# State-space scan: one direction's decay rows by broadcast transfers and a VectorE bound, the other's by TensorE products

## The reference

```
    acum = jnp.cumsum(loga.reshape(bsz, nc, CHUNK, ng, r), axis=2)
...
    alast = acum[:, :, -1]
    wgt = jnp.exp(alast[:, :, None] - acum)
...
        return (jnp.exp(al_c)[..., None, None] * s
                + jnp.einsum('bjgn,bjgr,bjgrp->bgrnp', bm_c, wgt_c, v_c))
...
    seg = jnp.exp(jnp.where(tril, acum[:, :, :, None] - acum[:, :, None], -jnp.inf))
    cb = jnp.einsum('bcign,bcjgn->bcijg', cm, bm)
    y_intra = jnp.einsum('bcijgr,bcjgrp->bcigrp', seg * cb[..., None], v)
    cdec = jnp.exp(acum)
...
        y = jnp.einsum('bign,bgrnp->bigrp', cm_c, s) * cd_c[..., None]
```

## Time and profile before

| | |
|---|---|
| median of 3 runs | 2175.74 us (2174.65 to 2176.6) |
| the profiled execution's own time | 2172.17 us |
| its span in the trace | 2170.4 us |
| PE busy | 1881.5 us (87%) |
| DVE busy | 805.8 us (37%) |
| ACT busy | 508.4 us (23%) |
| POOL busy | 333.5 us (15%) |

### The profile page before, as it was taken

The page is one execution under the profiler, slowest core; times in us unless marked ns, Lnnn a source line. Parts: engine busy times, 40 slices in busy tenths (PEclk is TensorE's granted clock), DMA queues, the critical chain, the costliest instruction groups (busy, mean ns, idle before and its releaser), DMA issues.

```text
span 2170.4 us, 32842 instructions
## 1 busy us (share of the span) xinstructions
PE 1881.5 (87%) x13986; PEld 1128.2 (52%) x13986; DVE 805.8 (37%) x1427; ACT 508.4 (23%) x1119; POOL 333.5 (15%) x323
## 2 busy tenths in 40 slices
PE   6999989999999988888899999989999975656565
PEld 3874667845875433333346566577888721212112
DVE  3331757655633010010126877667764300000001
ACT  2451421343012100000023323454442200000001
POOL 1431044422320000000013000045540000000000
PEclk9999999999999999999999999999999998878788
DMA  9321051230239999999993432300004699999997
GB/s 385 144 88 69 9 197 78 97 136 1 87 146 394 430 426 429 429 430 431 428 411 140 198 155 105 142 2 2 2 2 175 257 429 430 429 430 428 430 431 296
DMA packets 46689, 528.05 MB, mean 243 GB/s; under 512 B 3409, under 2 KB 7761, under 8 KB 23121
## 3 DMA queue, kind: packets, MB, share of 16 engines
q1 hardware_dynamic: 44784, 522.56, 57.7%
q10 hardware_dynamic: 1760, 3.42, 0.4%
HBM read 524.91 MB, written 1.05 MB: 242 GB/s over the span
## 4 chain that ended last, share of the span: by engine, by line
PE 53%; DMA 28%; DVE 11%; issue 2%; ACT 2%; DVEq 1%; POOLq 1%; POOL 0%; ACTq 0%; PEld 0%; SPq 0%; PEldq 0%
DMA ring<-in_moe_w 27%; PE bank L1453 12%; PE bank L715 8%; PE bank L826 7%; PE bank L1335 4%; PE bank L1004 3%; PE bank L794 3%; DVE x L2303 2%; PE bank L1037 2%; PE bank L1060 1%; DMA ring<-in_mod_w 1%; DVE x L2891 1%; PE bank L969 1%; DVE ring L2432 1%; PE bank L633 1%
## 5 line engine op out<-in xcount | busy, mean ns | idle before, releaser
L1453 PE MATMUL bank<-ring,xgs 128*32 128x512 f32 x2984 | 375.7, 658 | 125.6 <-DMA ring<-in_moe_w 124.2
L1453 PEld LDWEIGHTS bank<-ring,xgs 128*32 128x32 f32 x2984 | 106.8, 119 | 367.3 <-issue 284.2
L1453 PE MATMUL bank<-ring,hT 128*32 128x512 f32 x1488 | 194.9, 678 | 72.8 <-DMA ring<-in_moe_w 72.8
L826 PE MATMUL bank<-hT,ring 128*128 128x256 f32 (+1 forms) x784 | 232.7, 454 | 2.0 <-ACT hT L1623 1.4
L2732 DVE SCALAR_TENSOR_TENSOR x<-bank,modT,x 128x256 f32<-128x256 f32 x96 | 42.4, 479 | 456.9 <-PE bank L1477 456.8
L826 PEld LDWEIGHTS bank<-hT,ring 128*128 128x128 f32 x784 | 146.6, 190 | 82.3 <-issue 66.8
L1453 PEld LDWEIGHTS bank<-ring,hT 128*32 128x32 f32 x1488 | 53.2, 122 | 200.8 <-issue 153.6
L2303 DVE SCALAR_TENSOR_TENSOR x<-gluR,cols,x 128x256 f32<-128x256 f32 x240 | 116.1, 484 | 16.6 <-issue 0.9
L715 PE MATMUL bank<-hT,ring 128*128 128x256 f32 x432 | 99.9, 381 | 4.1 <-ACT ssd_g L1674 2.2
L715 PEld LDWEIGHTS bank<-hT,ring 128*128 128x128 f32 x432 | 81.1, 190 | 18.1 <-issue 6.2
L3123 POOL MEMSET gluR<- 128x3008 f32 x1 | 2.6, 2612 | 497.4 <-DVEq L2742 497.4
(11 more groups left out here) (578 smaller groups left out, 3051.0 us busy)
## 6 DMA issues: line engine op xcount, KB each, us to landing
ring<-in_moe_w SPq DMA_DIRECT2D x56, 4096.0 KB, 22.5
ring<-in_moe_w SPq DMA_DIRECT2D x28, 2048.0 KB, 20.9
ring<-in_moe_w SPq DMA_DIRECT2D x55, 1024.0 KB, 14.4
ring<-in_mod_w SPq DMA_DIRECT2D x12, 4096.0 KB, 13.5
ring<-in_moe_w SPq DMA_DIRECT2D x12, 3072.0 KB, 21.9
ring<-in_cd_w SPq DMA_DIRECT2D x6, 4096.0 KB, 14.1
ring<-in_ab_w SPq DMA_DIRECT2D x5, 4096.0 KB, 19.9
ring<-in_ab_wo SPq DMA_DIRECT2D x2, 4096.0 KB, 13.9
```

What stands on the lines that cost most here:

```text
L826: last = mm(ps[p["no"] % 4][:, p["c0"]:T], w[:, k, :], hT[:, k, p["c0"]:T], start=(k == 0), stop=(k == KD - 1))
L1453: last = mm(ps[banks + s][32 * j:32 * j + 32, :], lhs[s][:, 4 * kh + k, 32 * j:32 * j + 32], piece(g, k, j), start=(kh == 0 and k == 0), s ...
```

## The change

The first direction's rows stay products of TensorE. The second direction's rows come by transfers: SP writes the 32 rows of acum of the second direction to a DRAM tensor `ssd_rows`, waits for that, and then reads each row back with a broadcast to all 128 partitions, straight into `mats` (16 transfers of 256 KB, two for each head pair; from k = 2 on after `outputs(k - 2)` is done). VectorE takes the minimum of each row and a value for each partition (`bounded`), ScalarE's exp then reads and writes `mats` in SBUF, and the far side of the diagonal is cut by a second version of cb, multiplied by a 0/1 mask `past`. `matrices` now goes by direction: the first direction of head pair k + 1 with `bounded(k + 1)` at q = 2, the second direction of k one step pair later, at q = 0.

```
+        def rows_out(sp):
+            sp.wait_ge(sg("gate_cums"), 1)
+            sp.dma_start(ssd_rows, ac[96:128, :]).then_inc(sg("dram_written"), 16)
+            sp.wait_ge(sg("dram_written"), 16)
+            sp.wait_ge(sg("gate_cums_turned"), 1)
+        def decay_rows(sp, k):
+            if k >= 2:
+                sp.wait_ge(sg("ssd_y"), k - 1)
+            for hp in range(2):
+                r = 2 * k + hp
+                sp.dma_start(mats[(4 * k + 2 + hp) % 8], ssd_rows[r:r + 1, :].broadcast_to([P, T])).then_inc(sg(f"ssd_row{k % 2}"), 16)
...
+                if (stage, i) == ("about", 4):
+                    rows_out(sp)
+                    decay_rows(sp, 0)
+                    decay_rows(sp, 1)
+                if (stage, i) == ("mod10", 0):
+                    for k in range(2, 8):
+                        decay_rows(sp, k)
...
-                    for d in range(2):
-                        u = 4 * k + 2 * hp + d
...
-                        mm(ps[(4, 5, 7)[u % 3]], ident[r, 64 + 32 * d + 2 * k + hp:65 + 32 * d + 2 * k + hp].broadcast_to([32, P]), ac[r, :],
-                           start=True, stop=False, tile_position=(64 + 32 * d, 0))
...
+                    u = 2 * k + hp
...
+                    mm(ps[(4, 5, 7)[u % 3]], ident[64:96, 64 + u:65 + u].broadcast_to([32, P]), ac[64:96, :],
+                       start=True, stop=False, tile_position=(64, 0))
+                    mm(ps[(4, 5, 7)[u % 3]].rearrange("p (t i) -> p t i", t=NT), identb[:, :], m_far[:, :].unsqueeze(1).broadcast_to([P, NT, P]),
+                       start=False, stop=True).then_inc(sg("ssd_bc"), 1)
...
+                            if d:
+                                act.wait_ge(sg("ssd_bounded"), 2 * k + hp + 1)
+                                row = m
...
             def ssd_gates():
-                for g in range(2):
-                    dve.wait_ge(sg("ssd_cb"), g + 1)
-                    V.tensor_copy(cbs[g], ps[4 + g]).then_inc(sg("ssd_cbm"), 1)
                 dve.wait_ge(sg("gate_cums_turned"), 1)
...
                 V.tensor_tensor(dtw[:, :, :], ps[2][:, 0:256].rearrange("p (t r) -> p t r", t=NT), acT[:, :, :], ALU.subtract).then_inc(sg("gate_gap"), 1)
+                for g in range(2):
+                    V.tensor_copy(cbs[g][0], ps[4 + g])
+                    V.tensor_tensor(cbs[g][1].rearrange("p (t i) -> p t i", t=NT), ps[4 + g].rearrange("p (t i) -> p t i", t=NT),
+                                    past[:, :].unsqueeze(1).broadcast_to([P, NT, P]), ALU.mult).then_inc(sg("ssd_cbm"), 1)
                 dve.wait_ge(sg("gate_exps"), 1)
...
+                def bounded(k):
+                    if k >= 8:
+                        return
+                    dve.wait_ge(sg(f"ssd_row{k % 2}"), 32 * (k // 2 + 1))
+                    for hp in range(2):
+                        m, r = mats[(4 * k + 2 + hp) % 8].rearrange("p (t i) -> p t i", t=NT), 32 + 2 * k + hp
+                        V.tensor_tensor(m, m, acT[:, :, r:r + 1].broadcast_to([P, NT, P]), ALU.min).then_inc(sg("ssd_bounded"), 1)
...
-                    if q in (1, 2):
-                        matrices(k + 1, q - 1)
+                    if q == 2:
+                        matrices(k + 1, 0)
+                        bounded(k + 1)
+                    if q == 0 and k >= 0:
+                        matrices(k, 1)
```

More of the change, by code:

```diff
@@ L899, in ssd_gates @@
                         tt = slice(t * P, (t + 1) * P)
-                        last = mm(ps[4 + g][:, tt], bmc[:, g, tt], cmc[:, g, tt], start=True, stop=True, skip_group_check=True)
-                    last.then_inc(sg("ssd_cb"), 1)
+                        mm(ps[4 + g][:, tt], bmc[:, g, tt], cmc[:, g, tt], start=True, stop=True, skip_group_check=True)
                 pe.wait_ge(sg("gate_cums"), 1)
@@ L917, in spreads @@
                         pe.wait_ge(sg("ssd_weights"), 1)
-                    for d in range(2):
-                        u = 4 * k + 2 * hp + d
[L920 to L924, removed]
-                        mm(ps[(4, 5, 7)[u % 3]], ident[r, 64 + 32 * d + 2 * k + hp:65 + 32 * d + 2 * k + hp].broadcast_to([32, P]), ac[r, :],
-                           start=True, stop=False, tile_position=(64 + 32 * d, 0))
[L927 to L930, removed]
+                    u = 2 * k + hp
+                    if u >= 3:
+                        pe.wait_ge(sg("ssd_decay"), 4 * ((u - 3) // 2) + (u - 3) % 2 + 1)
+                    elif u == 2:
+                        pe.wait_ge(sg("mod_added"), 3)
+                    mm(ps[(4, 5, 7)[u % 3]], ident[64:96, 64 + u:65 + u].broadcast_to([32, P]), ac[64:96, :],
+                       start=True, stop=False, tile_position=(64, 0))
+                    mm(ps[(4, 5, 7)[u % 3]].rearrange("p (t i) -> p t i", t=NT), identb[:, :], m_far[:, :].unsqueeze(1).broadcast_to([P, NT, P]),
+                       start=False, stop=True).then_inc(sg("ssd_bc"), 1)
                 def item_kv(v):
@@ L2013, in ssd @@
                 for k in range(8):
[L2014 to L2019, removed]
+                    for d in range(2):
+                        for hp in range(2):
+                            m, r = mats[(4 * k + 2 * d + hp) % 8], 32 * d + 2 * k + hp
+                            if d:
+                                act.wait_ge(sg("ssd_bounded"), 2 * k + hp + 1)
+                                row = m
+                            else:
+                                act.wait_ge(sg("ssd_bc"), 2 * k + hp + 1)
+                                if k >= 2:
+                                    act.wait_ge(sg("ssd_y"), k - 1)
+                                row = ps[(4, 5, 7)[(2 * k + hp) % 3]]
                             for t in range(NT):
-                                last = A_(mats[u % 8][:, t * P:t * P + P], ps[(4, 5, 7)[u % 3]][:, t * P:t * P + P], ACT.Exp,
-                                          bias=nacT[:, t, r:r + 1])
+                                last = A_(m[:, t * P:t * P + P], row[:, t * P:t * P + P], ACT.Exp, bias=nacT[:, t, r:r + 1])
                             last.then_inc(sg("ssd_decay"), 1)
```

33 lines of the change are left out of this document (19 added, 14 removed).

## The result

| | kernel before | changed kernel |
|---|---|---|
| median of the runs | 2174.57 us (20 runs, 2169.74 to 2177.79) | 2179.37 us (20 runs, 2177.50 to 2184.83) |
| profiled execution: time, span | 2172.17, 2170.4 us | 2178.58, 2176.9 us |

The ratio is 1.0026, 95% interval [1.0020, 1.0032]: 4.8 us by the medians, slower, at the edge of the 0.2% that the prediction took as the least difference that can be told (the interval begins there). The forecast was 2177.1 and no change. The time lies in the forecast's range, but the loss is more than three times the +1.4 us of the sum, and by the profiled executions most of it has a cause that no term of the sum held.

The account below looks back on a forecast made before the run. TensorE's own instruction row and VectorE's scale at each state item were taken to bound the scan. -1.26 + 2.65 = +1.4 us on the median 2175.74 gave 2177.1 us, range 2173.0 to 2183.0, called no change.

Parts of the forecast that it names:

- +1.4 us of the sum: Whole kernel: 1.26 us gained by the last item_add and 2.65 lost at the scan's end, all later stages moving along.
- Saving per spread: TensorE's spreads: only one bfloat16 pass is saved, 0.21 us each, since the two directions' float32 products run in parallel.
- Rival 2: TensorE's spreads: a lone 32-row product is quicker, saving 0.74 us a spread and giving 2171.3 us; chance 0.07.
- The walk on VectorE: Scan items: v = 1 0.8 us earlier, v = 2 level, v = 4 1.1 late, v = 7 level, last item_add 1.26 earlier.
- The end of the scan: First sum of squares: ScalarE's square comes 5.3 us after item_add, TensorE after 2.7, so TensorE stalls 2.6 us.
- I count no difference: ScalarE's second-direction exps: reading SBUF instead of PSUM was taken to cost no extra time.
- Rows, gates, GpSimd: Row transfers land in 3.3 us on an idle queue; 2.56 us of gate work hides in VectorE's wait; GpSimd allows VectorE a turn.
- rival 1: Row transfers land late, bounded holds up VectorE and the scale, some 7 us in all, 2184 us; chance 0.12.
- rival 3: Scale for v = 10: GpSimd's two instructions shut VectorE out, up to 2.33 us later, 2179.4 us; chance 0.11.

Follow-up runs that it names:

- f4_after_again: The changed kernel run again with nothing edited, source of the second profiled execution (2174.27 us); median 2180.13 us, ratio 1.0023 to the kernel before.
- e4_lone: Kernel before with the second direction's float32 spread product left out and another exp bias, no minima or row transfers; 2174.60 us, ratio 1.0002.
- g3_q3: Changed kernel with ScalarE's squares moved ahead of the last exps, 6 spare products before the scan, and minima behind VectorE's scales; 2168.02 us, ratio 0.9971.
- e2_tail: Changed kernel with ScalarE's squares 0 to 3 put ahead of the second direction's last eight exps; 2173.66 us, ratio 1.0001 to the kernel before.

## Why the prediction went as it did

- **Saving per spread.** Right: in f4_after_again and e4_lone the lone product keeps 1.05 us, and one mask pass goes. Rival 2 fell.
- **The walk on VectorE.** Right in mechanism and nearly in size: in the second execution v = 2 lost 0.9 of the 1.22 us that v = 1 had gained, v = 4 lost a further 0.9, and from v = 7 on 1.34 us came back (1.26 predicted). It stands 0.4 us better than forecast from v = 1 on and 0.7 from v = 7 on; why was not traced. That the minima ahead of the scale are the cause is shown by g3_q3.
- **The end of the scan.** Right: 2.8 us of wait against 2.6 (the terms give 5.31 - 2.71 = 2.60; the sum took 2.65). The term "I count no difference" for exps from SBUF was off: eight took 2.45 us against 2.18 from PSUM, about the difference. e2_tail shows that ScalarE's order alone makes the wait.
- **Rows, gates, GpSimd.** Rows landed in 3.3 and 3.6 us at the median for 3.3, and no wait of VectorE for them shows, so rival 1 fell. The queue was not always idle, as the prediction had it: a weight load of 4 MB followed the first four rows, and one of them took 6.2 us. Rival 1's price was added up wrong, too: five places at 1.8 us are 9, not 7. The Trainium skill (DMA: Bandwidth & Descriptors, Anatomy of one DMA) gave an estimate of 2.6; the measurement decides. Beside GpSimd's pair VectorE's pair took 3.79 us and the scale then waited 0.61 for TensorE, not for GpSimd, so rival 3 fell; that VectorE got its turn between two instructions (its pair ended at 513.50, GpSimd's at 515.70) agrees with the Trainium skill (SBUF — State Buffer, SBUF: two separate sides).
- **The step that failed** is the sum itself, "-1.26 + 2.65 = +1.4 us", with the sentence that every following stage moves with the scan. It counted each instruction at the clock of the rows of before and had no term for a clock that falls. Behind the 2.8 us wait the next products ran at half clock in both executions, 1.6 us more: +0.83 at the first sum became +2.41 at the mean. In the first execution falls at 439.7 and 467.0 cost 5.5 us more: +7.93. The profiled times agree with both: 2174.27 and 2178.58 stand 2.1 and 6.4 above the 2172.17 of before (the first execution came to its first spread 0.8 us earlier than the kernel before and was 0.7 shorter behind the mean: 7.93 - 0.8 - 0.7 = 6.4). The 4.8 us between the medians lie between the two; that the runs mix such executions fits this, but only the profiled ones show it.
- **Luck.** That 2179.37 still lies in the range is in part luck. The range reached to 2183.0 for late rows, which did not come, and the median of 3 runs that the sum was added to, 2175.74, lay 1.2 us above the 2174.57 of 20. By the difference, +1.4 was forecast and +4.8 measured.

What stays open: what decides, from one execution to the next, whether the clock falls at a given gap. That a wait of TensorE stood ahead is all that these rows show. The width of the lone product is undecided, and so is whether the change makes falls at the scan's start likelier: the kernel before has the same wait there and was profiled only once without the filler.

## What to carry to other kernels

An edit that takes work off TensorE, or makes it wait in a new place, is costed twice: once at the clock of the rows, and once with the products behind each gap at half clock. Where the gaps cannot go, spare products that end inside a wait cost little, if their passes are counted; here they went with a kept clock at the gap that they filled, not at later ones. When an in-order engine gets new work, put it behind the instruction that the bound engine waits for: here moving each head pair's two minima and four squares, with six spare products, turned 0.26% slower into 0.29% faster.

## What the hardware showed that I had not expected

- The same program ran the start of the scan at 1.2 GHz in one profiled execution and at 2.4 GHz in another, behind the same wait of 1.53 us, and the two scans stood 5.5 us apart.
- A wait of 2.8 us went with half clock within 1.2 us of its end in six profiles of six, with 1.6 us or more lost; waits of 0.9 to 1.7 us only sometimes.
- Eight exps of 128 columns took 2.45 us from SBUF, in place, and 2.18 from PSUM.
